# The expert sums of 32 tokens in a two-block transformer kernel: element gathers moved behind each set's row gathers, and the row sums moved and spread

## What is computed

```python
def block(args):
    xc, ec, gc = args
    u = jnp.take(expert_down, ec, axis=0)
    hdn = jax.nn.gelu(jnp.einsum('ted,td->te', u, xc))
    vsel = jnp.take(expert_up, ec, axis=0)
    return jnp.einsum('te,ted->td', gc * hdn, vsel)
```

## Time and profile before

| | |
|---|---|
| Median of three runs | 3057.23 us (3053.94 to 3062.21) |
| Profiled execution, its own time | 3048.75 us |
| Its span, first to last instruction | 3046.9 us |
| Granted TensorE clock, mean | 0.995 of full |
| Busy: TensorE, VectorE, ScalarE, GpSimd | 99%, 64%, 48%, 27% of the span |
| Expert up phase, by the trace | from about 1265 to about 1930 us |

### The profile page before, as it was taken

The page is one execution under the profiler, slowest core; times in us unless marked ns, Lnnn a source line. Parts: engine busy times, 40 slices in busy tenths (PEclk is TensorE's granted clock), DMA queues, the critical chain, the costliest instruction groups (busy, mean ns, idle before and its releaser), DMA issues.

```text
span 3046.9 us, 44468 instructions
## 1 busy us (share of the span) xinstructions
PE 3014.3 (99%) x16695; PEld 2673.0 (88%) x16695; DVE 1948.9 (64%) x2517; ACT 1474.8 (48%) x1794; POOL 808.6 (27%) x595
## 2 busy tenths in 40 slices
PE   9999999999999999999999999999999999999998
PEld 8999888888888888989999999999978888888887
DVE  5445564688875555658888876655786555555554
ACT  6445454555564444534444444554555434444443
POOL 3110000188888887232444500000000000000000
PEclk9999999999999999989999999999999999999999
DMA  7764467577777778868999975554445666656664
GB/s 228 246 208 138 148 215 251 189 208 208 209 206 218 213 213 280 286 203 287 345 334 333 343 264 199 186 186 137 141 143 182 194 193 190 192 189 191 192 192 153
DMA packets 223182, 657.59 MB, mean 216 GB/s; under 512 B 57115, under 2 KB 60837, under 8 KB 222640
## 3 DMA queue, kind: packets, MB, share of 16 engines
q1 hardware_dynamic: 157696, 549.79, 55.5%
q0 software_dynamic: 60096, 88.67, 10.5%
q10 hardware_dynamic: 5232, 16.97, 1.5%
HBM read 617.16 MB, written 38.13 MB: 215 GB/s over the span
## 4 chain that ended last, share of the span: by engine, by line
PE 97%; DVE 1%; ACT 1%; issue 1%; DMA 0%; ACTq 0%; DVEq 0%
PE ps L1949 14%; PE ps L2243 12%; PE ps L2090 8%; PE ps L2092 8%; PE ps L2091 8%; PE ps L1927 8%; PE ps L1928 8%; PE ps L1929 8%; PE ps L1948 8%; PE ps L2242 6%; PE ps L1945 1%; PE ps L2256 1%; PE ps L2255 1%; PE ps L2257 1%; PE ps L2239 1%
## 5 line engine op out<-in xcount | busy, mean ns | idle before, releaser
L687 DVE TENSOR_TENSOR w_lo<-raw,w_hi 128x1024 fp32r<-128x1024 f32 (+2 forms) x1072 | 1275.6, 1194 | 891.7 <-ACT w_hi L682 860.7
L682 ACT ACTIVATE w_hi<-raw 128x1024 fp32r<-128x1024 f32 (+2 forms) x1072 | 1107.8, 1035 | 1286.2 <-PE ps L1929 340.7
L1949 PE MATMUL ps<-x_all,w_hi 128*128 128x512 f32 x1920 | 667.6, 390 | 0.0
L1948 PE MATMUL ps<-x_all,w_lo 128*128 128x256 f32 x1920 | 541.5, 282 | 0.0
L2243 PE MATMUL ps<-acts,w_hi 128*128 128x448 f32 x1680 | 534.2, 378 | 5.0 <-issue 5.0
L552 POOL DMA_INDIRECT gates<-srch x256 | 492.1, 1922 | 154.2 <-issue 77.8
L2242 PE MATMUL ps<-acts,w_lo 128*128 128x224 f32 x1680 | 446.3, 266 | 1.9 <-issue 1.9
L2090 PE MATMUL ps<-w_hi,x_all 128*128 128x440 f32 (+2 forms) x1152 | 435.9, 378 | 0.4 <-DVE w_lo L687 0.4
L1949 PEld LDWEIGHTS ps<-x_all,w_hi 128*128 128x128 f32 x1920 | 360.5, 188 | 74.7
L2092 PE MATMUL ps<-w_hi,x_all 128*128 128x440 f32 (+2 forms) x1152 | 424.5, 368 | 0.0
L2091 PE MATMUL ps<-w_lo,x_all 128*128 128x440 f32 (+2 forms) x1152 | 424.3, 368 | 0.0
(11 more groups left out here) (390 smaller groups left out, 3460.1 us busy)
## 6 DMA issues: line engine op xcount, KB each, us to landing
raw<-in_peer_down SPq DMA_DIRECT2D x256, 512.0 KB
raw<-in_peer_up SPq DMA_DIRECT2D x256, 512.0 KB
raw<-in_w_mlp_in SPq DMA_DIRECT2D x128, 512.0 KB
raw<-in_w_mlp_out SPq DMA_DIRECT2D x128, 512.0 KB
raw<-in_w_in SPq DMA_DIRECT2D x112, 440.0 KB
raw<-in_w_in SPq DMA_DIRECT2D x96, 428.0 KB
raw<-in_w_out SPq DMA_DIRECT2D x64, 512.0 KB
gates<-zero POOLq DMA_DIRECT2D x32, 512.0 KB, 5.2
```

The source lines that it names most:

```text
L682: act.activation(w_hi[:, c % RING, 0:2 * n], raw[:, c % RING, 0:2 * n], ACT.Copy).then_inc(hi_made, 1)
L687: nc.vector.tensor_tensor(w_lo[:, c % RING, 0:2 * n], raw[:, c % RING, 0:2 * n], w_hi[:, c % RING, 0:2 * n].bitcast(F32), ALU.subtract).th ...
L1948: mm(o[:, 0], wl, xh, start=False, stop=False)
L1949: last = mm(o, wh, both, start=False, stop=(k == KT - 1))
```

## The change

Each element gather is taken out of the block of 32 and put behind the four row gathers of its set; for sets 0 to 2, whose rows are gathered earlier, the element gather stands where the block of 32 stood. It raises the semaphore of its set's buffer, which therefore counts 80 and not 64 for each use. `weigh` multiplies one column for one set, one chunk ahead of the set's first half, and waits for the set's five gathers; the first half of a set waits only for `weigh`. The sets begin at chunk 16 in place of 44 and follow each other every 6 chunks in place of 5: `weigh(s)` at 16 + 6s, the halves at 17 + 6s and 19 + 6s, the last half at chunk 205 in place of 201. `SETS_BY` is fitted to that.

```diff
-FIRST_SET, SET_EVERY = 44, 5
-SETS_BY = (3, 3, 6, 13, 19, 26, 32, 32)
+FIRST_SET, SET_EVERY = 16, 6
+SETS_BY = (3, 6, 11, 16, 22, 27, 32, 32)
...
+            def gather_hidden(s):
+
+                nc.gpsimd.indirect_dma_start(
+                    pk_hid[:, s:s + 1], None, hid_rows,
+                    bass.IndirectOffsetOnAxis(ap=pk_at[:, s:s + 1].bitcast(U32), axis=0)).then_inc(gathered[s % GBUF], 16)
...
                 if r == 1:
                     pool.wait_ge(spilled, 16 * 4 * PEER_ROUNDS)
-                    for s in range(TG):
-                        nc.gpsimd.indirect_dma_start(
-                            pk_hid[:, s:s + 1], None, hid_rows,
-                            bass.IndirectOffsetOnAxis(ap=pk_at[:, s:s + 1].bitcast(U32), axis=0)).then_inc(hid_gathered, 16)
+                    for s in range(done):
+                        gather_hidden(s)
                 while r and done < SETS_BY[r]:
                     gather_rows(done)
+                    gather_hidden(done)
                     done += 1
...
-            def weigh():
-
-                dve.wait_ge(hid_gathered, 16 * TG)
-                V.tensor_tensor(coef, pk_hid, pk_gate, ALU.mult).then_inc(coef_made, 1)
-                dve.wait_ge(coef_made, 1)
+            def weigh(s):
+
+                dve.wait_ge(gathered[s % GBUF], 80 * (s // GBUF + 1))
+                V.tensor_tensor(coef[:, s:s + 1], pk_hid[:, s:s + 1], pk_gate[:, s:s + 1], ALU.mult).then_inc(coef_made, 1)
...
-                dve.wait_ge(gathered[s % GBUF], 64 * (s // GBUF + 1))
+                dve.wait_ge(coef_made, s + 1)
...
-                if pos == FIRST_SET - 1:
-                    weigh()
                 s, at = divmod(pos - FIRST_SET, SET_EVERY)
-                if 0 <= s < TG and at in (0, 2):
-                    add_rows(s, at // 2)
+                if 0 <= s < TG:
+                    if at == 0:
+                        weigh(s)
+                    if at in (1, 3):
+                        add_rows(s, at // 2)
```

More of the change, by code:

```diff
@@ L352, in build @@
         hid_turned, hid_back, hid_full = sem("hid_turned"), sem("hid_back"), sem("hid_full")
-        packed, pieces_made, hid_gathered, coef_made = sem("packed"), sem("pieces_made"), sem("hid_gathered"), sem("coef_made")
+        packed, pieces_made, coef_made = sem("packed"), sem("pieces_made"), sem("coef_made")
         gathered = [sem(f"gathered{i}") for i in range(GBUF)]
```

## The result

| | before | after |
|---|---|---|
| Median of the timed runs | 3059.38 us (3052.59 to 3062.21, 6 runs) | 3031.89 us (3031.36 to 3032.49, 6 runs) |
| Profiled execution, its own time | 3048.75 us | 3031.99 us |
| Its span | 3046.9 us | 3030.2 us |
| Granted TensorE clock, mean | 0.995 | 0.999 |

The ratio is 0.9931, 95% interval 0.9913 to 0.995: faster by 0.7%, clear of the noise. The two profiled executions differ by 16.8 us, where 17.2 were worked out. The medians differ by 27.5 us.

A forecast was written before the change was run, and what follows sets the result against it. TensorE, busy 3014.3 of 3046.9 us, was taken as the bound; losses of 16.0 and 1.2 us go, other terms zero: 3057.2 - 17.2 = 3040.0 us median (3031.5 for a profiled execution), range 3030 to 3060.

The forecast's parts named there:

- both losses: TensorE's gaps in the up phase: 16.0 us at 1305 to 1330 us, 1.2 us at 1627 to 1629 us.
- No series is longer than five to ten gathers, 7 to 14 us: GpSimd's unbroken gathers after the change; the old series that hurt were 46 and 17 us.
- the 8.5 us: Median of the runs of before above the profiled execution; unexplained by the trace and kept in the forecast.
- The forecast's own range: 3030 to 3046 us, chance 0.68; gaps may vary by run, and half of the 8.5 us may be more of them.
- The first: Rival: gaps belong to a place in TensorE's program or an accident; 16.0 us kept, 3056 to 3057 us; chance 0.2.
- The second: Rival: each element gather costs 0.5 us wherever it stands; half, 8 us, comes back, 3048 us; chance 0.08.
- The third: Rival: VectorE waits for the five sets that come first after brings, landing late; 3068 us; chance 0.04.
- the 5.7 allowed: VectorE: 31 more `weigh`s at 0.18 us each, 5.7 us at most, covered by its idle time; zero cost.
- The page on separate ports: Counter-argument: DMA and compute engines have separate SBUF ports, so a gather could not hold up TensorE; sum would be 0.
- Traffic: DMA beside the up phase: 325 GB/s after, 339 before, both below the harmless 410; zero cost.
- GpSimd's pauses: Expected sign in the profile after: GpSimd pauses on `rows_used` after every set.
- ScalarE's late chunks: ScalarE starts chunks 17 to 20 late, released by "remote"; read as showing that data are not lacking.

The follow-up runs named there:

- the first experiment: The kernel after with the start, spacing and sets by round of the kernel before: 3042.4 us, ratio 0.9979.
- the kernel with the block kept: The kernel before with six chunks to a set from chunk 32, block of 32 element gathers unchanged: 3049.17 us, ratio 1.0003.

## Why the prediction was right

**The loss and its cause.** "I take both losses as gone: -17.2 us" held: the pair of profiles gives 16.8 us, in the two stretches named. That the cause is the unbroken series was only argued from two places; the runs show it from both sides. The block in four pieces takes the loss away with nothing moved, and a series added elsewhere brings it back. "No series is longer than five to ten gathers, 7 to 14 us" came out to the gather: the longest is ten in 14.2 us.

**Which half of the change does it.** The prediction counted the series of both halves and took the new spacing into the sum, but did not ask what the move alone would do. The expectation of the first experiment did, and had it wrong, with 3031 to 3034 us. Five gathers to a set make the series behind the brings 15 long in the old schedule, and these cost 10 us. The spacing of six chunks, by which only one or two sets are allowed at the end of the brings, is what keeps them at five to ten.

**The mis-sized term: the 8.5 us left in place.** "I leave the 8.5 us where they are: the trace doesn't say what they were." They were, as far as the runs show, more of the same loss. The six runs of after agree within 1.1 us; the six of before lie 20.7 to 30.3 us above their median, while the profiled execution of before had lost only 16.8. The gaps may begin early or late in the same series: 27.7 us in for the earlier trace rows, 14.3 us in where 26.6 us were lost. No profile of before at 3060 us was taken, so for its own runs this stays an inference; the kernel with the block kept shows it directly, at 3058.73 us. The forecast's own range left room for half of the 8.5 us; all of it went, and the median came out 8 us below the 3040.0 forecast. The spread of the first three runs of before, 8 us, was itself a sign that something in them varies; it could be read as part of the loss only once the kernel after repeated to 1.1 us.

**Rivals.** The first, that the gaps belong to a place or an accident, falls with the added series. The page "Runtime: NRT & Kernel Launch" of the Trainium skill, section "Instruction fetch mechanics", has an engine's instructions refilled in blocks of 16 KiB. A stall of that kind would stay where the blocks are fetched; here the gaps came to a stretch without a fetch, and the trace has the same 106 fetches in all. The second, 0.5 us for each element gather wherever it stands, falls with one in flight and with the memsets between: 32 gathers, nothing lost. The third, VectorE waiting for sets, has no trace. VectorE of the kernel after, in order of time at `weigh(0)`, and its groups from 1270 to 1760 us:

```profile
1299.67 1.23 DVE L692 TENSOR_TENSOR w_lo<-raw,w_hi 128x1024 fp32r<-128x1024 f32 x1 [1.28 <-ACT w_hi L687]
1300.82 0.15 DVE L1503 TENSOR_TENSOR big<-big 128x1 f32<-128x1 f32 x1
```

```profile
L692 DVE TENSOR_TENSOR w_lo<-raw,w_hi 128x1024 fp32r<-128x1024 f32 x197 | 240.0, 1222 | 77.6 <-ACT w_hi L687 66.1 <-issue 9.4
...
L1513 DVE SCALAR_TENSOR_TENSOR row_sum<-big,row_sum 128x1024 f32<-128x1024 f32 x60 | 76.7, 1279 | 0.0
...
L1503 DVE TENSOR_TENSOR big<-big 128x1 f32<-128x1 f32 x31 | 4.8, 154 | 0.0
```

No idle time before a `weigh` or before the halves at L1513, and 0.15 us for each `weigh`, 4.8 us in all beside the 5.7 allowed.

**The page on separate ports.** The page "SBUF — State Buffer" of the Trainium skill, section "SBUF: two separate sides", says that a DMA and a compute engine can't slow each other. As far as traffic goes the runs agree with it: 96 direct DMAs cost TensorE nothing. As a rule that nothing of a DMA's reaches TensorE it doesn't hold here: 32 gathers of single elements cost 24 us. What the rows show late is the start of matmuls and the news of their end (see below); whether a port has a part in it, no run shows.

**Traffic.** The zero was right, but what was named as its sign did not come. "DMA should stay under 400 GB/s for longer stretches" does not hold: of the stretches of 20 us after, one has 405, others 395, 387 and 386. One of them:

```profile
1600.00:1620.00 20.00, 20.00 (x130) 19.10 (x129) 14.80 (x15) 8.44 (x9) 9.89 (x8) 1.00 1.03 405
```

130 matmuls start in it, no fewer than elsewhere, so full queues are not what costs. The means of 325 and 339 GB/s say nothing of the stretches in which brings and a set meet.

**GpSimd's pauses.** They came after nearly every set. GpSimd's waits of the kernel after, 1270 to 1840 us:

```profile
POOL big L561 <- DVE row_sum L1513: 156.0, 24, 9.9
```

**What comes first.** The prediction read ScalarE's late chunks as a second sign of the same gaps; they come ahead of them. ScalarE's chunk 17 waits for TensorE's chunk 13. The last matmuls of chunks 13 and 14 in the kernel before:

```profile
1299.84 0.38 PE L2243 MATMUL ps<-acts,w_hi 128*128 128x448 f32 x1
1302.34 0.38 PE L2243 MATMUL ps<-acts,w_hi 128*128 128x448 f32 x1
```

In steady chunks ScalarE starts 0.47 us behind such a start. Chunk 17 starts 2.40 us behind the first and chunk 18 8.42 us behind the second, while TensorE keeps its pace until 1305.7 us. So the news that TensorE has finished a chunk is late before any matmul is. The same holds in all eight series with gaps that were profiled. By the semaphore records in the traces, TensorE's signal to ScalarE first comes 2.0 to 3.5 us behind the modelled end of a chunk, where it is 0.02 us in steady chunks; ScalarE then misses its turn 5.5 to 7.1 us ahead of TensorE's first gap. The last landing on record of the load that ScalarE also waits for is earlier in each case, so it isn't a load that is late.

**What stays open.** Nothing here shows what ties a long series of GpSimd's indirect DMAs to these signals and to TensorE's issue. One rival to a cause in the program's own work is untested: the recording of the execution. The trace loses records where indirect DMAs follow each other quickly. From 1760 to 1800 us the traces with 96 direct DMAs and with memsets hold 272 records of landings of weights (16 for each of 17 loads), the one with a gather in flight at a time 266, and the two with a break behind every eight gathers 119 and 152, though these lose no time; the one with the bare 32 holds 40, for about half as many loads. The timed runs, too, each have a span and a granted clock on record, and no run shows what an execution takes that isn't recorded. So the loss is shown for executions as they were measured here, and not beyond them.

Nor is it settled why the gaps begin 14 to 28 us into one series, while one of 15 over 22.8 us,' 12 from 1449 us on and the 12 from 1197 us on do no harm. The rows give a hint. GpSimd of the kernel with 32 added gathers, in order of time, up to the first gap at 1772.66 us:

```profile
1757.54 2.80 POOL L662 DMA_INDIRECT big<-hid_rows,big  x1 [0.30 <-issue]
1760.64 0.95 POOL L662 DMA_INDIRECT big<-hid_rows,big  x1 [0.30 <-issue]
...
1770.67 0.95 POOL L662 DMA_INDIRECT big<-hid_rows,big  x1 [0.30 <-issue]
1771.93 1.81 POOL L662 DMA_INDIRECT big<-hid_rows,big  x1 [0.30 <-issue]
```

Now and then an issue takes 1.3 us or more in place of 0.95, and here nine quick ones stand between two slow ones just ahead of the first gap. In the eight series with gaps that were profiled, eight or nine quick ones (up to 1.13 us) stand ahead of the gaps in seven. In the harmless series of 15 there are never more than three in a row, in the longest of after seven. That looks like something that fills while gathers come at their quickest and empties in a slow issue or a break. But in the kernel with the block kept and six chunks to a set the gaps begin after six, a slow one and four more, and the earlier trace rows' harmless series has eight in a row of up to 1.10 us at its end. It is a reading of rows, and no run tried it. None of the eleven kernels is faster than the change by more than its own spread.

## What to carry to other kernels

Where a saturated engine shows gaps without a releaser inside work whose data are there, look for what another engine's queue was doing (and, as this case leaves open, for what the recording may add), and whether the gaps end with it; then break that up before moving it. Here three waits in a series of 32 indirect DMAs gave what a new schedule gave, and moving the gathers without the schedule gave a third of it (4.4 of the 14.8 us between 3046.81 and 3032 us): count how many come unbroken after each move, behind every wait that lets a backlog go. And ask of a spread between runs whether it is part of the loss and not noise around it: here 10 us of spread shrank to 1.1 when the loss went.

## What the chip showed that was not expected

- From 14 to 28 us into some series of GpSimd's indirect DMAs, 1.25 to 1.4 us apart, until about their end, TensorE starts matmuls 0.7 us apart or more, again and again; the granted clock of the stretches shown was 0.55 to 0.97. TensorE's signals to ScalarE are late 5.5 to 7.1 us before that. 32 cost 16 to 27 us by profile, 16 cost 7 at the median. Gathers of rows do it as well as gathers of elements.
- 96 direct DMAs on the same queue (50.8 us), 32 memsets (28.8 us), 32 gathers one at a time (4.6 us each), and 32 with a break of 2 us behind every eight cost nothing that can be measured.
- The direct DMAs are issued in 0.54 to 0.59 us each, the indirect ones in 1.13 to 1.14 us on average plus 0.3 us between two.
